# Gated delta scan: diagonal blocks of both directions inverted in one pass on 128 partitions

## The reference

```python
decay = exp(where(tril_incl, g[..., :, None] - g[..., None, :], -inf))
lmat = where(tril_strict, einsum('bnhid,bnhjd->bnhij', k_beta, k) * decay, 0.0)
t_inv = triangular_solve(eye + lmat, eye)          # unit lower triangular inverse
u = t_inv @ v_beta
w = t_inv @ (k_beta * exp(g))
...
v_new = u_i - w_i @ state
o_i = (q_i * exp(g_i)) @ state + a_i @ v_new
state = state * exp(g_last) + (k_i * exp(g_last - g_i)).T @ v_new
```

## Time and profile before

| | |
|---|---|
| median of three runs | 2976.65 us |
| the profiled execution | 2969.94 us |
| its span in the trace | 2968.2 us |
| PE / DVE / ACT / POOL busy over the span | 91% / 47% / 35% / 20% |
| mean granted clock of TensorE | 0.945 |
| first fill matmul, first x_base matmul, last matmul of the scan | 553.3, 620.6, 1254.3 us |

### The profile page before, as it was taken

One profiled execution on the slowest core, in us unless ns is written; L12 is line 12 of the kernel. 1 busy time (PEld: TensorE's weight loads), 2 busy tenths in 40 slices (PEclk: granted clock), 3 DMA queues, 4 the chain that ended last, 5 costly groups with the idle time before them and its releaser, 6 DMA issues. The chain is left out here.

```text
span 2968.2 us, 46123 instructions
## 1 busy us (share of the span) xinstructions
PE 2691.4 (91%) x18134; PEld 2530.2 (85%) x18134; DVE 1406.6 (47%) x2321; ACT 1040.6 (35%) x1801; POOL 601.8 (20%) x488
## 2 busy tenths in 40 slices
PE   7999999899899999728999868989999999999999
PEld 3898999788788888726777758889999999999999
DVE  4564332156667676447888833352222242222222
ACT  4212333234234343136778733332222222222211
POOL 1001222334333433133223221210111000111100
PEclk9999999989779899858999989999999999999999
DMA  5324664343343332140000044332222233222232
GB/s 202 144 80 131 220 220 158 125 117 95 90 138 86 97 101 72 58 164 14 9 17 16 12 180 167 116 98 71 78 76 72 78 114 94 71 78 71 69 96 70
DMA packets 195643, 294.22 MB, mean 99 GB/s; under 512 B 82800, under 2 KB 121744, under 8 KB 193936
## 3 DMA queue, kind: packets, MB, share of 16 engines
q1 hardware_dynamic: 192592, 276.15, 29.9%
q10 hardware_dynamic: 2880, 15.73, 1.5%
HBM read 228.28 MB, written 63.52 MB: 98 GB/s over the span
## 5 line engine op out<-in xcount | busy, mean ns | idle before, releaser
L277 PE MATMUL f_ps<-mf_h_hi,mf_w_hi 128*128 128x320 f32 x1408 | 435.1, 309 | 1.4 <-PEq L1985 1.4
L277 PE MATMUL f_ps<-mf_h_hi,mf_w_lo 128*128 128x320 f32 x1408 | 435.1, 309 | 0.0
L277 PE MATMUL f_ps<-mf_h_lo,mf_w_hi 128*128 128x320 f32 x1408 | 435.1, 309 | 0.0
L2418 DVE TENSOR_TENSOR mf_w_lo<-mf_w_raw,mf_w_hi 128x1024 fp32r<-128x1024 f32 (+1 forms) x135 | 188.9, 1399 | 431.7 <-ACT mf_w_hi L2270 431.4
L277 PE MATMUL proj_ps<-h_hi,w_hi 128*128 128x320 f32 x896 | 282.9, 316 | 6.0 <-DVE w_lo L571 5.6
L277 PE MATMUL proj_ps<-h_lo,w_hi 128*128 128x320 f32 x896 | 278.2, 311 | 0.0
L277 PE MATMUL proj_ps<-h_hi,w_lo 128*128 128x320 f32 x896 | 278.1, 310 | 0.0
L277 PEld LDWEIGHTS f_ps<-mf_h_hi,mf_w_hi 128*128 128x128 f32 x1408 | 264.4, 188 | 1.6 <-issue 1.6
L277 PEld LDWEIGHTS f_ps<-mf_h_lo,mf_w_hi 128*128 128x128 f32 x1408 | 264.4, 188 | 0.0
L277 PEld LDWEIGHTS f_ps<-mf_h_hi,mf_w_lo 128*128 128x128 f32 x1408 | 264.4, 188 | 0.0
L2344 POOL TENSOR_TENSOR f_ff_lo<-f_ff_f,f_ff_hi 128x640 f32 (+1 forms) x44 | 69.3, 1575 | 783.4 <-ACT f_ff_hi L2270 783.4
(11 more groups left out here) (321 smaller groups left out, 6434.2 us busy)
## 6 DMA issues: line engine op xcount, KB each, us to landing
mf_w_raw<-w_up_dram SPq DMA_DIRECT2D x88, 512.0 KB, 3.5
w_raw<-w_in_dram SPq DMA_DIRECT2D x48, 512.0 KB, 4.3
w_ada_raw<-w_ada_dram SPq DMA_DIRECT2D x16, 1024.0 KB, 5.0
mf_w_raw<-w_mix_dram SPq DMA_DIRECT2D x32, 512.0 KB, 4.8
mf_w_raw<-w_down_dram SPq DMA_DIRECT2D x32, 448.0 KB, 3.3
delta_t<-delta_tile ACTq DMA_DIRECT2D x10, 1024.0 KB, 6.7
decay_t<-g_rows SPq DMA_DIRECT2D x40, 256.0 KB, 4.5
kq_t<-delta_t SPq DMA_DIRECT2D x20, 512.0 KB, 4.5
```

The source lines that it names most:

```text
L277: ins = nc.tensor.matmul(out, w(k), a(k), start=(first and n == 0 and q == 0), stop=(last and n == len(ks) - 1 and q == 2))
L2418: nc.vector.tensor_tensor(wlo[:, slot, 0:nk], raw[:, slot, 0:nk], whi[:, slot, 0:nk].bitcast(F32), ALU.subtract).then_inc(E[half]["lo"], 1)
```

## The change

The direction pair 2j, 2j+1 is now inverted in one pass on 128 partitions, 64 for each direction; the backward blocks are transposed on load by ScalarE (`turn_backward`), and the result of the pair is stored in four pieces. It is done in odd units only, one piece in each level (`BASE_AT`). For this the products are made three units ahead (`AHEAD`), in the first half of their level (`K_AT`), and the lists begin at unit -4; `n_t` and `attn_t` have five buffers for four. k and q are loaded twice, for the products (`kq_t`, two buffers for four) and again for the recurrent step (`kq_again`). The inverse is loaded in 8 pieces of twice the size; in even units that is early, in odd ones it follows the pair's store. The opening has 6 matmuls per slot in four units, and its fill alternates between bank_F and a half of banks_bc (`fill_bank`) up to the 13th half tile. `o_stage` and `fill_stage` have one buffer for two.

```diff
-        K_AT = {(LV[1], 1): 0, (LV[2], 1): 1}
+        K_AT = {(LV[1], 0): 0, (LV[2], 0): 1}
-        UNITS = range(-3, NU + 1)
+        UNITS = range(-AHEAD - 1, NU + 1)
...
-        BASE_ROWS = ((1, 2, 3, 4, 5), (6, 7), (8,), (9,))
+        BASE_AT = {LV[0]: (1, 2, 3, 4, 5), LV[1]: (6, 7, 8), LV[2]: (9,)}
...
-                return 12 if u == -1 else 6
+                return 6
...
+        OPENING = 13
+        fill_bank = lambda t, g: (BC[1][:, 1] if 2 * t + g < OPENING and g else FB)[:, 0:GN]
...
             def blocks_out(k):
+                if k >= 2:
+                    sp.wait_ge(e["blocks_in"], 32 * (k // 2))
                 sp.wait_ge(e["a_out"], a_index["k", k, 1, 1] + 1)
...
+            def blocks_in(j):
+                if j:
+                    sp.wait_ge(e["base_step"], BASE * j)
+                sp.wait_ge(e["blocks_out"], 256 * (j + 1))
+                for d, to in ((0, dg), (1, db)):
+                    sp.dma_start(to[64 * d:64 * d + 64], io["diag"][d].rearrange("b h j i -> (b h) (j i)")).then_inc(e["blocks_in"], 16)
+
+            def inverse_out(j):
+                sp.wait_ge(e["xo_ready"], 2 * j + 2)
+                if j:
+                    sp.wait_ge(e["xb_in"], 128 * 2 * j)
+                for d in range(2):
+                    for x in range(2):
+                        dst = io["diag_inv"][d, :, x ^ d].rearrange("b h i j -> b h (i j)")
+                        sp.dma_start(dst, xo[64 * d:64 * d + 64, x].bitcast(F32)).then_inc(e["pair_out"], 16)
...
             def inverse_in(k):
-                sp.wait_ge(e["pair_out"], 16 * (k + 1))
+                sp.wait_ge(e["pair_out"], 64 * (k // 2 + 1))
...
-                    for x in range(2):
-                        sp.dma_start(XB[rows, x, :, rows].bitcast(F32), io["diag_inv"][b, :, x].rearrange("h i j -> i h j")).then_inc(e["xb_in"], 16)
+                    sp.dma_start(XB[rows].rearrange("p x h i -> p (x h) i")[:, :, rows].bitcast(F32), io["diag_inv"][k % 2, b].rearrange("x h i j -> i (x h) j")).then_inc(e["xb_in"], 16)
...
-                if has(u + 1):
-                    inverse_out(u + 1)
-                    if u == -1:
-                        sp.wait_ge(e["xb_zero"], 1)
+                if has(u + 1) and u % 2 == 0:
                     inverse_in(u + 1)
...
+                if has(u + 1) and u % 2:
+                    inverse_out((u + 1) // 2)
+                    if u == -1:
+                        sp.wait_ge(e["xb_zero"], 1)
+                    inverse_in(u + 1)
...
+            def turn_backward(j):
+                act.wait_ge(e["blocks_in"], 32 * (j + 1))
+                if j:
+                    act.wait_ge(e["base_step"], BASE * j)
+                nc.scalar.activation(dg[64:128].rearrange("p (i j) -> p i j", i=16), db[64:128].rearrange("p (i j) -> p j i", i=16), ACT.Copy).then_inc(e["turned_in"], 1)
...
             def body(u):
+                if has(u + 1) and u % 2:
+                    turn_backward((u + 1) // 2)
...
-                    if has(u + 1) and lv == LV[1]:
-                        inverse_pair(u + 1)
-                    if has(u + 3) and lv in (LV[1], LV[2]):
-                        decay(u + 3, lv - LV[1])
+                    if has(u + 1) and u % 2 and lv == LV[2]:
+                        inverse_pair((u + 1) // 2)
+                    if has(u + AHEAD + 1) and lv in (LV[1], LV[2]):
+                        decay(u + AHEAD + 1, lv - LV[1])
...
-                    if has(u + 1) and i < 2:
-                        diagonal(u + 1, BASE_ROWS[2 * i])
-                        diagonal(u + 1, BASE_ROWS[2 * i + 1])
-                    fill(u, 3 * i)
-                    for c in range(2):
-                        if has(u + 2) and (lv, c) in K_AT:
-                            products(u + 2, K_AT[lv, c])
-                        fill(u, 3 * i + 1 + c)
+                    if has(u + AHEAD) and (lv, 0) in K_AT:
+                        products(u + AHEAD, K_AT[lv, 0])
+                    if has(u + 1) and u % 2:
+                        diagonal((u + 1) // 2, BASE_AT[lv])
+                    for s in range(3 * i, 3 * i + 3):
+                        fill(u, s)
...
+                    n = 2 * t + g
+                    if lo == 0 and n > 1:
+                        pe.wait_ge(e["fill_out"], n if n >= OPENING else n - 1)
```

More of the change, by code:

```diff
@@ L822, in delta_scan @@
                         z_index[u, lv, c] = len(z_index)
-                    if has(u + 2) and (lv, c) in K_AT:
+                    if has(u + AHEAD) and (lv, c) in K_AT:
                         for odd in range(2):
-                            a_index["k", u + 2, K_AT[lv, c], odd] = len(a_index)
+                            a_index["k", u + AHEAD, K_AT[lv, c], odd] = len(a_index)
             for c in range(2):
@@ L938, in _ @@
             for u in UNITS:
-                if has(u + 3) and u >= -1:
-                    load_rows(u + 3)
+                if has(u + AHEAD + 1) and u + AHEAD + 1 >= 2:
+                    load_rows(u + AHEAD + 1)
                 reload(u, 0)
@@ L945, in _ @@
                     load_kv(0)
+                    load_again(0)
                 if has(u + 1) and u >= 0:
@@ L976, in _ @@
                     fill(u, s)
-                if has(u + 2):
-                    blocks_in(u + 2)
+                if has(u + AHEAD) and (u + AHEAD) % 2:
+                    blocks_in((u + AHEAD) // 2)
                 reload(u, 3)
             sp.wait_ge(e["kept"], 64)
-            for i in range(2):
-                sp.wait_ge(o_stored[i], 16 * NT)
-                sp.wait_ge(f_stored[i], 16 * (NF // 2))
+            sp.wait_ge(o_stored, 16 * NU)
+            sp.wait_ge(f_stored, 16 * NF)
         @block.gpsimd
@@ L1272, in products @@
                     a = a_index["k", k, c, m % 2]
[L1273 to L1274 removed]
+                    both = kq[half(h), k % 2, :, (h // 2) * P:(h // 2 + 1) * P]
+                    ins = mm(A[a % 2][:, 256 * (m // 2):256 * (m // 2) + 256].rearrange("p (t i) -> p t i", t=2), kT(kq, k, h // 2)[half(h)], both)
                     if m >= 2:
@@ L1307, in body @@
                             last.then_inc(e["z_ps"], 1)
-                        if has(u + 2) and (lv, c) in K_AT:
-                            products(u + 2, K_AT[lv, c])
+                        if has(u + AHEAD) and (lv, c) in K_AT:
+                            products(u + AHEAD, K_AT[lv, c])
                         fill(u, 3 * i + 1 + c)
@@ L1317, in body @@
                         for m in range(H4):
-                            last = mm(bank(a)[:, m], NTf[:, u % 4, c, m], XX[:, c, 0, m].bitcast(F32), False, m == H4 - 1)
+                            last = mm(bank(a)[:, m], NTf[:, u % RING, c, m], XX[:, c, 0, m].bitcast(F32), False, m == H4 - 1)
                         last.then_inc(e["a_ps"], 1)
```

138 lines of the change are left out of this document (68 added, 70 removed).

## The result

The changed kernel takes **2997.27 us** (median of 11 runs, 2989.16 to 3006.02) against 2976.69 us for the kernel before on the same chip (11 runs): ratio **1.0063, 95% interval [1.0047, 1.0079]**. It is slower by 0.63% where 2957 us was forecast, and it lies outside the range. The profiled execution took 2997.56 us, its span is 2995.8 us with a granted clock of 0.936 (before 0.945).

What follows compares the result with a forecast made beforehand. VectorE's list was taken to set each unit's middle level, PE's own work the rest. Terms -2.8, -2.5, -7.7, -1.4, -3.0 and -1.7 summed to -19 us, giving 2957 us for the median; range 2915 to 2992.

Steps and rivals of the forecast that it cites:

- opening and unit 0: Fill and first unit: second bank removes ScalarE waits, unit 0 starts later but runs without diagonal work; together -1.7 us.
- units 1 to 4: Scan units at the steady pair time, plus 3.5 us for unit 4 where fill runs out: 123.7 against 126.5, -2.8 us.
- units 5 and 6: Scan units without fill: unit 5 stays late through SP's state wait, unit 6 gains its waits; 69 against 71.4, -2.5 us.
- units 7 to 16: Scan units put at 300.5 us against 308.2, -7.7 us.
- units 17 and 18: Late scan units that lose the products, 2.2 us each: 55.7 against 57.1, -1.4 us.
- unit 19: The last unit starts without a stand of PE before it: -3.0 us.
- The steady pair: Odd unit 31.0 us with PE's 3.9 us stand, even unit 26.6, slow clock 2.5: 60.1 us per pair.
- the turn: ScalarE's added step at odd units' head, waiting for blocks_in: costs nothing, blocks there 26 to 30 us into the even unit.
- Rival 3: SP's x_base queue, odd units: eight loads take as long as sixteen; 4.2 us at ten places, 2999 us, chance 0.20.
- Rival 2: Inverse's return path on SP some 4 us shorter, neither stand nor slow clock: 64 us less, 2893 us, chance 0.17.
- Rival 4: VectorE's saved time only traded: PE's even-unit waits return for ScalarE's x_inv, or slow clock takes the gain; 2976, chance 0.13.
- What would show it: Signs in the profile: no attn_t waits, diagonal work in odd units alone, x_base waits of 3 to 5 us before nine units.

Runs made afterwards that it cites:

- experiment 1: The change with SP loading the pair's blocks right behind their stores and storing unit 3's state later, at the unit's end: 2983.23 us, ratio 1.0029.
- e3_both: The change with both the blocks loaded right behind their stores and diagonal row 9 back in the middle level: 2950.82 us, ratio 0.9895.
- experiment 5: e3_both with the four reloads of h of units 5 and 6 issued together at each unit's head on SP: 2940.12 us, ratio 0.9873.
- e8: e3_both with VectorE's diagonal rows ahead of the products in a level: 2926.65 us, ratio 0.9845.
- e9: e8 with the reloads of h of units 5 and 6 at each unit's head on SP: 2920.51 us, ratio 0.9822.
- e2: The change with diagonal row 9 back in the middle level, ScalarE's pair and SP's inverse transfers moved with it: 2963.2 us, ratio 0.9949.
- e12: e9 with GpSimd's n_t_eye of an odd unit held until VectorE's first diagonal rows are done: 2916.29 us, ratio 0.9795.
- e4: The kernel before with the products in the first half of their level, on VectorE ahead of the diagonal rows: 3017.86 us, ratio 1.0127.
- e5: The kernel before with TensorE's products in the first half of their level, on VectorE behind the diagonal rows: 3000.52 us, ratio 1.0081.

## Why the prediction was wrong

The sum, term by term, against the profiled execution of before:

| term | forecast | measured |
|---|---|---|
| opening and unit 0 | -1.7 | +5.0 |
| units 1 to 4 | -2.8 | +1.0 |
| units 5 and 6 | -2.5 | +8.3 |
| units 7 to 16 | -7.7 | +21.8 |
| units 17 and 18 | -1.4 | -2.0 |
| unit 19 | -3.0 | -2.9 |
| sum | -19 | +31 |

The medians differ by 21 us and not 31: the span of the two profiled executions differs by 27.6, with 3.6 us less outside the scan, and that of before was 7 us below its median. The forecast for the median, 2957, was missed by 40.

- *The steady pair was right.* "A pair of units is then 31.0 + 26.6 + 2.5 = 60.1 us": units 9 and 10 take 60.9, 15 and 16 60.7. "PE stands 3.9 us before each even unit": 3.5 to 5.4. The marks inside unit 9 too: pair done at 22.3 us (21.7), stores from 22.3, loads 26.5 to 30.3, last landed at 31.7 (31.0).

```profile
960.25 2.52 SPq L907 DMA_DIRECT2D diag_inv<-diag_inverse_pair  x4
964.44 3.76 SPq L915 DMA_DIRECT2D x_base<-diag_inv  x8
```

- *The step that failed is the turn.* It was put at nothing with the words that the blocks "are there near the unit's end, 26 to 30 us. If they came later than 3 us into the odd unit, the copies would be late next". They landed 30.2 us after the start of unit 8, but 31.9, 38.8, 39.0 and 35.6 after that of 0, 4, 6 and 10, and the turn ran 4.5, 13.2, 7.1 and 6.4 us into units 1, 5, 7 and 11. For the copies behind it TensorE stood 1.3 us in unit 1 (with 17 us at the lower clock behind it), 11.0 in unit 5 and 3.2 in unit 11; in unit 7 the reload of h, next point, covered the late turn. Two things were left out. The landing of blocks_in had no figure of its own, and here it is 3.5 us behind 512 KB loads. And the wait of SP for the state and its stores was noticed ("now holds up ScalarE's turn") but priced as if it still held only the diagonal copy. In unit 5 the price is the standing; its clock of 0.64 is not, for it was 0.71 before and 0.63 in experiment 1, without the stand. In unit 11 it is 3.2 us of standing and a clock of 0.74, against 0.98 in experiment 1. Units 5 and 6 are 10.8 us over the forecast, units 11 and 12 (71.9) 11.8; experiment 1 takes 10.3 us off unit 5 and as much off unit 11.
- *The reload of h was not looked at.* It is not in any term. TensorE waited 0.5 us for it at unit 7 before, 6.7 in the change, 9.0 in e3_both, and units 7 and 8, 74.4 us, are 14.3 over the forecast; experiment 5, on top of e3_both, takes 13.1 us off unit 7. SP issued the last part hardly later than before, 34.0 us after the start of unit 6 against 33.5. But unit 6 had become 3.9 us shorter, 31.9 against 35.8, and that part took 6.4 us to land where TensorE had been served 4.8 us after the issue. The time saved in unit 6 ran into a transfer that had been 0.5 us from being the bound, and only a look at what is due next would have shown it.
- *What is left open.* In medians the blocks' way gave back 14 us of the miss of 40 and the reload 11 (in e3_both). The opening holds 6.7 us of it. Some 8 us no run repairs by itself; unit 1 is part of them, 39.8 us against the forecast's 33.5. Experiment 1 took only 2.0 off it: a wait of 0.8 us stayed, and a clock of 0.79, and what would lift that is open.
- *The opening was mis-sized.* The fill did get its second bank, and its waits for ScalarE fell from 9.8 to 3.0 us, but one of 3.2 for attn_t is new, and it ended at 617.9, not near 611. Unit 0 started at 629.0 instead of 623.5. The blocks landed at 604.9 and not 602, and the diagonal rows and what stands between them took until 618.0, 13 us, where 10.5 were allowed. The profile puts the stand of 11.14 us before the first x_base product down to GpSimd's n_t_eye; the last x_base load, issued near 626.9 and 1.9 us to landing in the median, came at about the same time, so which of the two ended it is not shown. Unit 0 then ran at a clock of 0.73 (0.72 before). In e8 and e9 it starts at 625.9 and 622.2.
- *Rival 3 is refuted though its number, 2999, is the one that came.* Eight issues of 16 KB took 3.76 us, 0.47 each, where sixteen of 8 KB took 0.53 each: twice the runs cost SP nothing there, nor in the nine other places where the path is bare (3.8 to 4.0 us for eight). Where the loads are issued early, in even units, eight took up to 7.8 us, and nothing waited for them. By the Trainium skill, DMA: Bandwidth & Descriptors, section Bandwidth, transfers under 64 KB are "descriptor-dominated"; the prediction read from it that the eight would take what the sixteen did, and this trace doesn't agree. The median from issue to landing went from 1.7 to 1.9 us. That the measured time is near 2999 is luck.
- *Rival 2*, the path covered, needed row 9 in the middle level. e2 has it: the stands vanish and even units take 26.6 us, as the forecast had them without a stand. The store that spoke for it, 2.2 us to landing, was of 128 KB and not 64.
- *Rival 4*, the saving only traded, doesn't hold for the even units, by the same 26.6. TensorE's waits for x_inv did rise from 8.5 to 27.4 us, but 15.5 of that are the three stands for the turn.
- *What would show it*: attn_t gone, VectorE's diagonal work in odd units alone and x_base stands of 3 to 5 us were seen. So was the last sign named, "if an odd unit shows ScalarE waiting for diag_products at its head, at the blocks' arrival".

## What to carry to other kernels

When a step is given a longer lead, follow the whole chain of transfers that feeds it through the issuing queue, unit by unit and not in the quiet unit alone: every wait and large load that the queue holds ahead of a small, urgent one is part of its price. And when a unit gets shorter, ask which transfer, timed by the old length, is now late. Here the change was right in its core, and the place of a few calls decided between 0.6% slower and 2% faster. After each repair look for the arrival that was hidden next; and put work that needs no partner into the time in which an engine waits for one.

## What was not expected of the hardware

- Tiny VectorE instructions on SBUF took 1.19 to 1.24 us instead of 0.16 to 0.17 while GpSimd ran n_t_eye, and the second of them ended at 879.93 where GpSimd had ended at 879.91. Over all ten places the first row's mean fell when GpSimd was held back, from e9 to e12, which differ in that alone:

```profile
L1182 DVE COPY diag_inverse<-diag_blocks 128x2 f32<-128x2 f32 x10 | 10.0, 997 | 10.0 <-ACT diag_blocks L1083 10.0
```

```profile
L1184 DVE COPY diag_inverse<-diag_blocks 128x2 f32<-128x2 f32 x10 | 3.6, 364 | 10.0 <-ACT diag_blocks L1085 10.0
```

- The two 64 KB block loads landed 3.5 us after issue where 512 KB loads went ahead of them, and 2.1 us where they went first, from the same queue.
- TensorE's granted clock fell to its lower level, 1.2 GHz, behind short waits, and for very different times: for 19 us (1007.2 to 1026.2) behind one of 3.2 us, for 17 us (from 664.3) behind one of 1.29, both in the change; for 3 us behind one of 1.37 (kernel before, at 1110.5), and not at all behind one of 1.39 (kernel before, at 1081.44). y_res waits of 1.9 to 2.4 us in e4 and e5 had 4 to 14 us of slow matmuls behind them. So a wait can be worth far more than its own length; the runs don't say how much in general.
